# Identity products in seven of TensorE's waits, and sixteen PEER dots moved from ahead of the later attention to behind it, in an encoder layer on one Trainium2 core

## The reference

```
sub-layer 1: h = adaLN(RMSNorm(x));  z = h @ w_in   (2048 -> GLU value | GLU gate | q | k | v)
   A: GLU -> causal depthwise conv (width 31) -> LayerNorm -> swish
   B: 16 heads of 64: chunked band attention with a relative-position bias
   x1 = x + gate * (concat(A, B) @ w_out)
sub-layer 2 (PEER): h2 = adaLN(RMSNorm(x1));  q = h2 @ w_pq  (8 heads)
   scores of two sets of 128 keys; the best 16 of 128 x 128 experts for each row and head
   dot = <h2 row, u_experts[pick]>;  out = sum over picks of weight(dot) * v_experts[pick]
final RMSNorm
```

## Time and profile before

| | us |
|---|---|
| median of 3 runs | 3935.77 (3933.07 to 3939.93) |
| the profiled execution | 3934.31 |
| its span in the trace | 3932.5 |

### The profile page before, as it was taken

One profiled execution on the slowest core, in us unless ns is written; L12 is line 12 of the kernel. 1 busy time (PEld: TensorE's weight loads), 2 busy tenths in 40 slices (PEclk: granted clock), 3 DMA queues, 4 the chain that ended last, 5 costly groups with the idle time before them and its releaser, 6 DMA issues.

```text
span 3932.5 us, 34350 instructions
## 1 busy us (share of the span) xinstructions
PE 3617.0 (92%) x12399; PEld 1919.4 (49%) x12399; DVE 2663.1 (68%) x4413; ACT 445.5 (11%) x975; POOL 1058.0 (27%) x881
## 2 busy tenths in 40 slices
PE   5899999997996889699989999999988899999996
PEld 1566545475543664365734444444465344444442
DVE  1258853158888877877976666766688764555766
ACT  2100005010000440101600000000052000000000
POOL 1000001215323444354242222222233422222331
PEclk8999999998998789899999999999999999999998
DMA  9877763659999999999799999999979999999997
GB/s 389 266 236 255 251 249 129 220 205 407 413 413 417 364 379 350 381 406 353 255 412 421 420 410 422 422 421 419 417 269 351 420 421 390 421 422 421 422 418 297
DMA packets 336705, 1411.15 MB, mean 359 GB/s; under 512 B 25849, under 2 KB 134369, under 8 KB 195582
## 3 DMA queue, kind: packets, MB, share of 16 engines
q0 software_dynamic: 119360, 840.83, 53.2%
q1 hardware_dynamic: 216176, 563.29, 37.8%
q10 hardware_dynamic: 1008, 4.98, 0.3%
HBM read 1383.50 MB, written 39.94 MB: 362 GB/s over the span
## 4 chain that ended last, share of the span: by engine, by line
DMA 50%; PE 26%; issue 14%; DVE 8%; POOL 2%; ACT 1%; SPq 0%; DVEq 0%; POOLq 0%; ACTq 0%
DMA R<-in_u_experts,MS 36%; DMA R<-in_v_experts,MS 10%; PE bank L875 8%; PE bank L906 7%; PE bank L1095 4%; DMA R<-in_w_ada 2%; DVE R L2269 2%; POOL R L762 2%; PE bank L821 1%; DVE R L2154 1%; DVE R L2061 1%; PE bank L1102 1%; PE bank L798 1%; DMA R<-in_w_in 1%; DMA R<-h_scratch 1%
## 5 line engine op out<-in xcount | busy, mean ns | idle before, releaser
L762 POOL DMA_INDIRECT R<-in_u_experts,MS x640 | 851.1, 1330 | 1690.3 <-DVE MS L2154 1407.4
L2154 DVE CUSTOM_DVE_ANT_0 R<-R 128x2048 f32<-128x2048 f32 x374 | 857.8, 2294 | 416.4 <-DMA R<-in_u_experts,MS 391.8
L1302 PE MATMUL bank<-R,RB 128*128 128x512 f32 x2304 | 1015.3, 598 | 47.4 <-DMA R<-in_v_experts 47.4
L1302 PE MATMUL bank<-RB 128*128 128x512 f32 x1792 | 778.2, 592 | 0.0
L1302 PEld LDWEIGHTS bank<-R,RB 128*128 128x128 f32 x2304 | 438.5, 191 | 614.2 <-issue 548.3
L2154 DVE CUSTOM_DVE_ANT_0 R<-R,RB 128x2048 f32<-128x2048 f32 x266 | 608.3, 2287 | 99.8 <-DMA R<-in_u_experts,MS 98.4
L1302 PEld LDWEIGHTS bank<-RB 128*128 128x128 f32 x1792 | 340.5, 190 | 428.6 <-issue 428.6
L2269 DVE SCALAR_TENSOR_TENSOR R<-R,MS 128x2048 f32<-128x2048 f32 x128 | 301.3, 2354 | 195.8 <-DMA R<-in_v_experts,MS 195.3
L875 PE MATMUL bank<-RB,R 128*128 128x256 f32 (+1 forms) x1536 | 400.8, 422 | 31.2 <-DMA R<-in_w_pq 23.5
L875 PEld LDWEIGHTS bank<-RB,R 128*128 128x128 f32 x1536 | 294.7, 194 | 130.2 <-DMA R<-in_w_pq 24.1
L1095 PE MATMUL bank<-RB,R 128*128 128x384 f32 x1024 | 337.4, 489 | 13.9 <-DMA R<-in_w_in 12.7
(11 more groups left out here) (357 smaller groups left out, 2207.0 us busy)
## 6 DMA issues: line engine op xcount, KB each, us to landing
R<-in_v_experts SPq DMA_DIRECT2D x144, 1024.0 KB, 9.2
RB<-in_v_experts SPq DMA_DIRECT2D x112, 1024.0 KB, 9.1
R<-in_w_ada SPq DMA_DIRECT2D x48, 2048.0 KB
R<-in_w_in SPq DMA_DIRECT2D x20, 2048.0 KB
R<-in_w_in SPq DMA_DIRECT2D x24, 1024.0 KB
R<-in_w_out SPq DMA_DIRECT2D x8, 2048.0 KB
R<-in_w_pq SPq DMA_DIRECT2D x8, 2048.0 KB, 10.5
R<-in_w_out SPq DMA_DIRECT2D x16, 1024.0 KB
```

The source lines that it names most:

```text
L762: pool.indirect_dma_start(dst, None, table, bass.IndirectOffsetOnAxis(ap=expert[T_ % 2][:, c:c + 1], axis=0)).then_inc(signal, 16)
L1302: x = pe.matmul(PB[4 * h + q][:, :], W[:, i, h * P:(h + 1) * P], vring[slot][:, q * PW:(q + 1) * PW], start=(i == 0), stop=(i == NKEY - 1))
L2154: V.tensor_tensor_reduce(u, u, x, 1.0, 0.0, ALU.mult, ALU.add, dots[t % 2][:, h * TOPK + s:h * TOPK + s + 1]).then_inc(dots_done, 1)
```

## The change

`stay_busy` is defined earlier, and called in seven places more: 4 products after the second turn of the modulation, 1 and 2 in the first attention, 5 after the first output projection, 14 in the scores of the later attention's first head (between the prompt's scores and the wait for `s_qx`), 13 and 8 before the last turns of the later tiles, and 11 in `build(1)`. Three of these stand behind a wait of their own (`o_free`, `s_h2E`). On DVE, `steps(124)` becomes `steps(108)`; `steps(8)` is added after the sixteenth head; and units v = 1 to 8 of the output projection take five dots instead of four. The total up to v = 9 is 208 dots in both (124 + 48 + 36, and 108 + 48 + 8 + 44).

```diff
@@ TensorE's program @@
             turn_mods(1)
+            stay_busy(3, 4)
...
             for h in range(3):
                 first_scores(h)
+                if h >= 1:
+                    stay_busy(6, h)
...
+            pe.wait_ge(o_free, 4 + 5)
+            stay_busy(0, 5)
             pe.wait_ge(o_free, 4 + 8)
...
                 pe.matmul(PB[2][:, 384:512], q[:, 256:384], k[:, NP:NT], start=True, stop=True)
+                if h == 0:
+                    stay_busy(5, 14)
                 pe.wait_ge(s_qx, hp + 1)
...
+            pe.wait_ge(o_free, 4 + 8 + 7)
+            stay_busy(3, 13)
             pe.wait_ge(o_free, 4 + 8 + 12)
             for t in range(TX, T):
                 if t == TX + 1:
                     pe.wait_ge(s_sq, 2 * T)
                 if t == TX + 2:
                     pe.wait_ge(s_h2E, 4 * (TX + 1))
+                    stay_busy(0, 8)
                 turn_h2(t, x1[t])
...
                 pe.wait_ge(tr_read, 2 * pair + 2)
+                if pair == 1:
+                    stay_busy(0, 11)
@@ VectorE's program @@
-            steps(124)
+            steps(108)
...
                 head_norm(h)
                 steps(2)
+            steps(8)
...
                 if v < 3 * TY:
-                    steps(4)
+                    steps(5 if v else 4)
```

More of the change, by code:

```diff
@@ L798, in tr, with stay_busy @@
                 return pe.transpose(out, in_, ident[0:k, 0:k])
+            def stay_busy(bank, n):
+                for i in range(n):
+                    pe.matmul(PB[bank][:, :], ident, ident.unsqueeze(1).to_broadcast([P, 4, P]), start=True, stop=True)
             pe.wait_ge(s_const, 1)
@@ L1271, in scatter @@
                 x.then_inc(oh_used, 1)
-            def stay_busy(bank, n):
-                for i in range(n):
-                    pe.matmul(PB[bank][:, :], ident, ident.unsqueeze(1).to_broadcast([P, 4, P]), start=True, stop=True)
             def build(pair):
```

## The result

| | before | changed |
|---|---|---|
| median of 20 runs each | 3935.33 us (3930.90 to 3945.54) | 3949.35 us (3932.75 to 3964.07) |
| profiled execution | 3934.31 | 3947.81 |
| its span | 3932.5 | 3946.0 |

The ratio is 1.0028, 95% interval 1.0018 to 1.0038: slower, as forecast, and 3 us from the predicted 3946. The profiled executions differ by 13.5 us, where the sum said 12. The sum came out by luck in part, as the profiles show stage by stage.

What follows compares the result with a forecast made beforehand. Each stage has its own bound: DMA engines full from 1220 on, TensorE or DVE nearly full in places. Terms -6 -20 -1 +36 +4 -1 = +12 on 3934.3 gave 3946 us, own range 3938 to 3956, over all cases 3922 to 3963.

Steps and rivals of the forecast that it cites:

- Start of the attention: Later attention's first maximum: queries ready sooner without 16 dots, bias in at about 1265 to 1270; -20 us (-14 to -25).
- The attention itself: Later attention, its 48 dots kept: warm clock shortens the first heads' sample scores; -1 us.
- Early sites: The 4, 1, 2 and 5 products: TensorE's half-clock rows run warm and move everything behind; -6 us (-1 to -9).
- The dots: Sixteen dots moved behind the attention: unit 9 comes +36 us later counted from the attention's end (+8 to +43).
- TensorE waits about 20 us for block 7, which DVE's longer queue covers: Output projection, eight dots in the wait: `w_out` block 7 arrives late, about 20 us, but DVE has work meanwhile.
- DVE's work alone less its idle time: Lower bound for the moved dots: eight at 2.29 us less 10.4 us of DVE idle time in units 1 to 8, +8.
- Together I count bytes: Sixteen row sets, 16.8 MB at 389 to 416 GB/s, take 40 to 43 us; idle engine time gives back 4.
- Third turn: Eight products ahead of the third turn make it start 3 to 10 us late, less 1.6 warm; +4 us (-2 to +8).
- Behind the turns I take the rest as rigid: After the third tile's turn: whatever that turn ends earlier or later, the whole kernel ends earlier or later.
- DVE's slack takes the dots: Rival, units 1 to 8: DVE's idle time absorbs dots, eight cost +8 instead of +36; 3918 us; chance 0.20.
- The loads are not held up: Rival: the eight dots' gathers fit unused DMA room, only the projection's 24.3 us count; 3934 us; chance 0.25.
- The products don't raise the clock: Rival: early sites give 0, attention's start -10, third turn +8; +34, some 3968 us; chance 0.15.

Runs made afterwards that it cites:

- second profile of before: The kernel before, unchanged, run and profiled once more; one run, 3933.7 us.
- products only: The kernel before with the seven groups of identity products added and the dots left where they were; ratio to before 0.9991 (0.9976 to 1.0006).
- products without the turns': Kernel before plus the identity products, dots unmoved, without the 13 and 8 ahead of the later turns; ratio to before 0.9995 (0.9985 to 1.0005).
- quarter rows: Kernel before with the change's dot moves, no identity products, sixteen of 48 gathers fetching 32 of 128 rows; ratio to before 1.0000 (0.9981 to 1.0019).

## Why the prediction came out, by its steps

**Start of the attention, -20: right in size, with another reason.** 21.0 us (24.8 against the second profile of before). The bias was in at 1260.9, ahead of the range given, and the fourteen products, not the bias, ended the wait. It was issued 24.9 us earlier, 6.9 of them because the block of `w_out` ahead was through sooner, and 18.1 because of the stores of new v rows, to which the prediction gave a bound and not the gain: between the block of `w_out` and the bias, their issues took 20.0 us of SP's queue before,

```profile
1257.56 12.07 SPq L492 DMA_DIRECT2D out_new_v_prompt<-RB  x2
1269.67 7.92 SPq L492 DMA_DIRECT2D out_new_v_sample<-RB  x1
```

and 1.9 in the changed kernel (last section). The gain shrank to 18.7 by the projection's first product, where -27 had been expected with the early sites.

**The attention itself, -1: no warm clock behind the first head.** The second and third heads' sample scores take 3.62 us each in the changed kernel, as before; from the first maximum to the sixteenth it took 157.8 us, 158.3 before.

**Early sites, -6: under-delivered, and did not last.** The clock rose: in the changed kernel's trace the first attention's scores take 0.70 us from the second head on where they took 1.22. From the first scores to dot 0 this gave 4.3 us, 3.7 in products only and 4.0 in products without the turns'. The first site gave nothing: its set of products took 19.99 us and not 19.59 (20.37 in the second profile of before), behind a wait of 6.57 us for its weights in which TensorE idled again. And the 4 us do not show at dot 0, which stands 0.1 earlier than before: in this profile the first scores began 4.1 us late (651.25 against 647.12; 1.1 and 0.3 late in the two others). What delayed them the runs don't say. Dot 107 then ended 1.9 later than before.

**The dots, +36: the direction right, the size and the reason partly wrong.** 43.3 us, at the upper bound of 43. Three statements failed. "TensorE waits about 20 us for block 7, which DVE's longer queue covers": the wait was 22.35, but DVE ran out of work and waited 7.7 for TensorE, and 17.1 where its queue was shorter. "DVE's work alone less its idle time", the lower bound of +8, took 2.29 us a dot and 10.4 us of idle time to put it in; a dot in the units is 2.6 us with its pieces of the search, and the idle time did not shrink but grew, to 15.8 us with eight dots more. And "Together I count bytes" took one price for all sixteen: 12.6 MB less gave 15.7 us where this price gives 31. The runs show two prices, a late block for the dots in the wait, and DVE's work with its waits for gathers for those in the units. Bytes gave 40 to 43 by another road. Of the signs, the block's wait (22.35, about 20 said) and units 0 to 9 (166.9, 155 to 165 said) came close, and the first unit came sooner, 38.1 us behind the attention's last product and not 41 to 46.

**Third turn, +4.** From unit 11 to the query products it cost 3.0 (29.5 against 26.5 us), and 4.3 in products only. In the change without the fourteen it took 34.2, but there DVE also waited 8.4 us for `mod_scratch`. The thirteen products cost nothing, as predicted, and gave nothing: TensorE idled 23.09 us behind them and the first turn took 3.68 us, 3.64 before.

**"Behind the turns I take the rest as rigid": wrong by 7 to 14 us.** The failure is that sentence; -1 was predicted behind it, and the profiles show -14.4 against the first of before and -7.5 against the second. From the query products to the end the thirteen profiles of this study range from 2249 (the change) to 2264 us (before, first profile; 2257 in the second). From dot 300 to the end they range from 1929 to 1937. So DVE's stream of dots and their gathers is nearer to rigid than TensorE's stages, though not exactly: its 8 us are as many as the range from unit 11 to dot 300, 348.2 (the change) to 356.2 (before; 354.0 in the second profile). At `build(1)` TensorE comes 22.5 us late and DVE, whose first stored row it needs there, 13.9 (2901.66 against 2887.79, DVE's timelines of the changed kernel and of before):

```profile
2901.66 1.87 DVE L2073 SCALAR_TENSOR_TENSOR R<-bank,MS 128x512 f32<-128x512 f32 x3
```

```profile
2887.79 1.86 DVE L2061 SCALAR_TENSOR_TENSOR R<-bank,MS 128x512 f32<-128x512 f32 x3
```

So 8.6 of TensorE's 14.80 us of wait are taken up, and the eleven products fill the rest and more. TensorE's timeline of the changed kernel:

```profile
2890.45 4.56 PE L803 MATMUL bank<-MS 128*128 128x512 f32 x10 [0.69 <-ACT RB L1614]
...
2895.70 9.71 PE L803 MATMUL bank<-MS 128*128 128x512 f32 x22
```

DVE's first of the three was done at 2902.3 and the products at 2905.4, so they stand some 3 us in the way. The page of the changed kernel agrees: its chain that ended last goes 54% over TensorE and 9% over gathers of u rows, where the other twelve have 25% to 31% and 27% to 36%. The +17.0 at dot 300 shrinks to +14.2 at the last dot all the same.

With the dots' +7, the 8 missing from the gains ahead of the projection, and these 14 back (+7, 3 and 7.5 against the second profile), the errors cancel: +12 predicted, +13.5 in the profile, and +11 by the ratio (7 to 15).

**The rivals.** "DVE's slack takes the dots" is out: eight dots in the units cost 26.6 us, not 8. "The loads are not held up" is out: block 7 was. "The products don't raise the clock" is out for the first attention and the third turn (1.91 us against 3.40), but that they gain nothing in all is not out: with the dots untouched the seven sites give 0.9991, with an interval (0.9976 to 1.0006) that contains no change.

## What to carry to other kernels

A free stretch on one engine is not free if what it starts there makes loads on another queue late: before moving gathered work into a wait, list what else must land in it, in the order of its queue, and ask which engine needs the last of it. When pricing moved work, take the whole busy time of the stretch over its number of steps, not the duration of the one large instruction. Before calling a tail rigid, find the stream whose distance to the end varies least over several profiles, and take a second profile of the kernel before: here the two differ by 7 us from the query products to the end, half of what one of them seemed to show. And when two edits touch the same wait, run each without the other: one may fill the wait that the other removes.

## What the runs showed of the hardware that I had not expected

The two kinds of queue took turns by packets, not by bytes or by need. In the first 37 us of the changed kernel's projection, the DMA view counts

```profile
q0 software_dynamic: 917, 6.63, 57.0%
q1 hardware_dynamic: 898, 5.79, 43.9%
```

917 packets of gathers and 898 of loads, and the gathers' are the larger by 12%. The Trainium skill ("DMA: Bandwidth & Descriptors", Queues, rings and completion order) says that each engine alternates between its queues packet by packet; the trace agrees, and also in the earlier trace rows, with 6600 and 6952 packets.

The busy share of the DMA engines did not tell how full they were: 0.97 stood beside 335 GB/s with the quarter rows and beside 389 in the earlier trace rows.

The SP queue's issues took long when gathers were in flight. The issues of the three stores of new v rows ahead of the first bias took 19.5 to 20.0 us in the four profiles with 124 dots ahead of the attention, 6.7 to 13.3 in the three with 116 or 118, and 1.8 to 4.3 in the six with 108, where the gathers had stopped earlier. The bias behind them waited for that. SP's queue in the changed kernel:

```profile
1250.69 0.98 SPq L492 DMA_DIRECT2D out_new_v_prompt<-RB  x2
1251.71 0.96 SPq L492 DMA_DIRECT2D out_new_v_sample<-RB  x1
1252.77 0.40 SPq L527 DMA_DIRECT2D RB<-ext_scratch  x1
```

The changed kernel's runs spread over 31 us and before's over 15, and the first head's last prompt score stood anywhere from 1234 to 1262 over the thirteen profiles, dot 107 from 1218 to 1240, though all have the same dots up to there. No order between the two shows. The runs don't say what decides how far each of the two streams has got.
